# A fused two-block transformer kernel: convolution operands on SyncE's queue, forgetting bias through memory

## The reference, cut to what matters

```
# band attention of block one, 12 heads, two per pair
s = einsum(q, k) * scale + bias ; p = softmax(where(valid, s, -inf)) ; out = p @ v

# convolution module of the even mixer: 512 channels, 31 taps
a  = u * sigmoid(gate)
y  = conv_general_dilated(a, w, padding=[(CONV_K - 1, 0)], feature_group_count=512) + b
yf = (y - mean(y)) * rsqrt(var(y) + EPS) * ln_g + ln_b ; out = silu(yf)

# forgetting attention of the odd mixer: 16 heads
c  = cumsum(log_sigmoid(zf + b_f))
sc = einsum(q, k) / sqrt(Dh) + c[t] - c[s]
p  = softmax(where(t >= s, sc, NEG)) ; out = p @ v
```

## Time and profile before

| what | before |
| --- | --- |
| median of 3 runs | 1598.29 us (1597.94 to 1598.76) |
| the profiled execution | 1599.74 us |
| its span, first to last instruction | 1598.0 us |
| TensorE busy | 1587.4 us, 99% |
| VectorE busy | 1092.2 us, 68% |
| ScalarE busy | 919.5 us, 58% |
| GpSimd busy | 56.2 us, 4% |
| DMA | 287.67 MB, mean 180 GB/s |

### The profile page before, as it was taken

One profiled execution on the slowest core, in us unless ns is written; L12 is line 12 of the kernel. 1 busy time (PEld: TensorE's weight loads), 2 busy tenths in 40 slices (PEclk: granted clock), 3 DMA queues, 4 the chain that ended last, 5 costly groups with the idle time before them and its releaser, 6 DMA issues.

```text
span 1598.0 us, 23594 instructions
## 1 busy us (share of the span) xinstructions
PE 1587.4 (99%) x9256; PEld 1354.9 (85%) x9256; DVE 1092.2 (68%) x1759; ACT 919.5 (58%) x1555; POOL 56.2 (4%) x96
## 2 busy tenths in 40 slices
PE   9999999999999999999999999999999999999998
PEld 7898888889788888888887788888888889888887
DVE  5986867778677768656677466567565667775665
ACT  6766645567655546545476664447444484664544
POOL 4000000000030000000002100000000000000000
PEclk9999999999999999999999999999999999999999
DMA  8545675554355565566655555655666564356662
GB/s 299 146 146 189 217 238 192 186 174 144 118 193 190 175 199 179 188 197 189 191 159 161 143 191 186 196 185 171 210 185 188 181 200 146 119 184 199 184 189 75
DMA packets 212401, 287.67 MB, mean 180 GB/s; under 512 B 11100, under 2 KB 180382, under 8 KB 212292
## 3 DMA queue, kind: packets, MB, share of 16 engines
q1 hardware_dynamic: 208676, 280.00, 55.3%
q0 software_dynamic: 3616, 6.17, 1.4%
HBM read 284.47 MB, written 3.87 MB: 180 GB/s over the span
## 4 chain that ended last, share of the span: by engine, by line
PE 97%; DMA 1%; ACT 1%; issue 0%; SPq 0%; DVE 0%; POOL 0%; DVEq 0%; ACTq 0%
PE two L2216 91%; PE two L2293 1%; PE two L2462 1%; PE two L2475 1%; PE two L2485 1%; PE two L2870 0%; DMA vals<-u_dram 0%; PE two L2279 0%; PE two L2488 0%; DMA raw<-in_mem_w_kv 0%; PE two L2626 0%; DMA raw<-in_ffn_w_up 0%; DMA u_dram<-aux 0%; PE two L2456 0%; PE two L2844 0%
## 5 line engine op out<-in xcount | busy, mean ns | idle before, releaser
L2216 PE MATMUL two<-act_parts,w_hi 128*128 128x512 f32 (+1 forms) x2784 | 801.7, 353 | 0.0
L1488 DVE TENSOR_TENSOR w_lo<-raw,w_hi 128x1024 fp32r<-128x1024 f32 (+1 forms) x520 | 613.1, 1221 | 105.8 <-ACT w_hi L870 105.6
L2216 PE MATMUL two<-act_parts,w_lo 128*128 128x256 f32 x2256 | 635.0, 281 | 0.0
L2216 PEld LDWEIGHTS two<-act_parts,w_hi 128*128 128x128 f32 x2784 | 487.0, 188 | 81.1 <-issue 5.3
L870 ACT CAST w_hi<-raw 128x1024 fp32r<-128x1024 f32 (+1 forms) x522 | 516.6, 1046 | 5.5 <-DMA raw<-in_ffn_w_up 5.0
L2216 PEld LDWEIGHTS two<-act_parts,w_lo 128*128 128x128 f32 x2256 | 425.5, 189 | 2.1
L2216 PE MATMUL two<-w_hi,act_parts 128*128 128x512 f32 (+2 forms) x832 | 248.6, 378 | 1.5 <-ACT w_hi L870 1.2
L999 ACT COPY p_sb<-two 128x512 f32<-128x512 f32 x108 | 62.4, 578 | 247.1 <-PE two L2216 247.1
L2216 PE MATMUL two<-w_hi,hid_even 128*128 128x512 f32 x576 | 187.8, 393 | 0.0
L2216 PEld LDWEIGHTS two<-w_hi,act_parts 128*128 128x128 f32 x832 | 150.2, 188 | 33.4 <-issue 3.6
L1616 DVE TENSOR_TENSOR pt_sb<-two,p_sb 128x512 f32<-128x512 f32 x54 | 37.3, 691 | 198.4 <-ACT p_sb L999 198.4
(11 more groups left out here) (318 smaller groups left out, 1198.8 us busy)
## 6 DMA issues: line engine op xcount, KB each, us to landing
raw<-in_ffn_w_up SPq DMA_DIRECT2D x160, 512.0 KB, 3.9
raw<-in_ffn_w_down SPq DMA_DIRECT2D x132, 512.0 KB, 3.5
raw<-in_ffn_w_gate SPq DMA_DIRECT2D x80, 512.0 KB, 3.7
raw<-in_a_w_in SPq DMA_DIRECT2D x24, 512.0 KB, 4.3
raw<-in_fox_w_in SPq DMA_DIRECT2D x20, 512.0 KB, 3.8
raw<-in_ffn_w_up SPq DMA_DIRECT2D x32, 256.0 KB, 3.5
raw<-in_w_kv SPq DMA_DIRECT2D x12, 512.0 KB, 3.8
raw<-in_a_w_out SPq DMA_DIRECT2D x8, 512.0 KB, 3.8
```

The costliest lines, as they stand in the source:

```text
L1488: nc.vector.tensor_tensor(w_lo[:, r, 0:n], raw[:, r, 0:n], w_hi[:, r, 0:n], ALU.subtract).then_inc(lo_done, 1)
L2216: return nc.tensor.matmul(dst, a, w, start=start, stop=stop, skip_group_check=True)
```

## The change

**Convolution.** `stack` and the tile `shift` are gone: all four chunks are turned (`turn_u(0)` to `turn_u(3)`), copied (VectorE takes 0 and 2, ScalarE 1 and 3), written to `u_dram` and read back. Writes and reads stand on SyncE's queue, chunks 0 and 1 ahead of the load of the seventh slot of the output weights, chunks 2 and 3 ahead of the third load of the next feed-forward part. `conv(2)` and `conv(3)` stand ahead of `swa_out(0)`, `conv(1)` is cut by `values("swa", 2)`, and the last pair's scores come after the projection.

**Forgetting attention.** For pairs 2 to 7 (`BY_ROWS = 2`) the product with `pick` is left out. GpSimd's `spread_gates` writes `rowc` to `c_dram`, loads each pair's rows spread over all partitions into one of four buffers, cuts the causal mask into it (two `affine_select` per pair) and signals `bias_ready`. VectorE's `scores` waits for that and adds this tile in place of the mask. The three engines' lists go by stages: values of pair n-2, turns of n-1, scores of n.

**Band attention.** Some calls change places: scores of pair 3 before values of pair 1, values of pairs 2 and 3 together, values of 6 and 7 together behind two more output chunks; ScalarE's and VectorE's lists follow. Some semaphores are merged, with counts to match.

```diff
# SyncE
+            def stack_two(c):
+                if c == 0:
+                    sp.wait_ge(pad_out, 16 * CCH)
+                for i in (c, c + 1):
+                    sp.wait_ge(u_taken[i], 1)
+                    sp.dma_start(u_dram[i * P:(i + 1) * P, UPAD:UPAD + SEQ], cv[:, i, :]).then_inc(u_out[i], 16)
+                for i in (c, c + 1):
+                    sp.wait_ge(u_out[i], 16)
+                    for g in range(4):
+                        sp.dma_start(stacked(i, g),
+                                     bass.AP(tensor=u_dram.tensor, offset=(i * P + g * GRP) * (UPAD + SEQ) + UPAD - CONV_K,
+                                             ap=[[1, 4], [UPAD + SEQ, GRP], [1, XW]])).then_inc(stacked_in[i], 16)
+
+            out_rows("swa", ab_w_out_2[0], {6: lambda: stack_two(0)})
+            ffn(3, ffn_w_gate_2[0, 1], 0, ffn_w_up_2[0, 1], 0, ffn_w_down_2[0, 1], early={2: lambda: stack_two(2)})
...
# GpSimd: write_u and read_stacked removed (the same transfers for chunks 1 to 3)
+            def spread_gates():
+                pool.wait_ge(gates_m, 2)
+                pool.dma_start(c_dram, rowc[0:FOX_H, :]).then_inc(bias_in[0], 16)
+                pool.wait_ge(bias_in[0], 16)
+
+                def load(i):
+                    if i >= 4:
+                        pool.wait_ge(h_max, PAIR0["fox"] + BY_ROWS + i - 3)
+                    wide = FOX_BIAS[i % 4].rearrange("p (h k) -> p h k", k=CAUSAL)
+                    for at, n_keys in ((0, P), (P, SEQ)):
+                        pool.dma_start(wide[:, :, at:at + n_keys],
+                                       bass.AP(tensor=c_dram.tensor, offset=2 * (BY_ROWS + i) * SEQ,
+                                               ap=[[0, P], [SEQ, 2], [1, n_keys]])).then_inc(bias_in[i % 2], 16)
+
+                load(0)
+                load(1)
+                for i in range(FOX_H // 2 - BY_ROWS):
+                    pool.wait_ge(bias_in[i % 2], (0 if i % 2 else 16) + 32 * (i // 2 + 1))
+                    for half in range(2):
+                        own = FOX_BIAS[i % 4][:, half * CAUSAL:(half + 1) * CAUSAL].rearrange("p (a k) -> p a k", a=3)[:, 0:3:2, :]
+                        ins = nc.gpsimd.affine_select(out=own, in_=own, compare_op=ALU.is_ge, fill=NEG, base=0,
+                                                      pattern=[[0, 2], [-1, P]], channel_multiplier=1)
+                    ins.then_inc(bias_ready, 1)
+                    if i + 2 < FOX_H // 2 - BY_ROWS:
+                        load(i + 2)
...
# VectorE, scores
+                    elif kind == "fox" and n >= BY_ROWS:
+                        dve.wait_ge(bias_ready, n - BY_ROWS + 1)
...
# TensorE, scores
-                    if kind == "fox":
+                    if kind == "fox" and n < BY_ROWS:
...
# TensorE, band attention
             scores("band", 2)
+            scores("band", 3)
             values("band", 1)
...
-            values("band", 6)
             turns("band", 7)
             band_out(3, 1)
             band_out(5, 0)
+            values("band", 6)
+            values("band", 7)
             band_out(4, 1)
-            values("band", 7)
+            band_out(5, 1)
...
# TensorE, convolution and sliding window
+            project("GU1", 0, {3: [lambda: turns("swa", 0)], 6: [lambda: turn_u(0), lambda: turn_u(1), lambda: turns("swa", 1), lambda: values("swa", 0)]})
-            stack(0)
             scores("swa", 2)
             values("swa", 1)
-            stack(1)
-            project("GU1", 1, {3: [lambda: scores("swa", 3)]})
+            project("GU1", 1)
+            scores("swa", 3)
             conv(0, 0, QUADS // 2)
             turns("swa", 2)
             turn_u(2)
             turn_u(3)
             conv(0, QUADS // 2)
-            conv(1)
+            conv(1, 0, QUADS // 2)
             values("swa", 2)
+            conv(1, QUADS // 2)
             turns("swa", 3)
             mean(0)
+            conv(2)
+            values("swa", 3)
             mean(1)
-            values("swa", 3)
+            conv(3)
+            mean(2)
             swa_out(0, 1, 0)
             swa_out(0, 0, 0)
-            conv(2)
-            conv(3)
-            mean(2)
             mean(3)
...
# TensorE, forgetting attention
+            def fox_stages(n):
+                if n >= 2:
+                    values("fox", n - 2)
+                if n >= 1:
+                    turns("fox", n - 1)
+                if n < 8:
+                    fox_scores(n)
```

More of the change, by code:

```diff
@@ L518, in build @@
         gates_em = sem("gates_em")
+        bias_in = [sem(f"bias_in{i}") for i in range(2)]
+        bias_ready = sem("bias_ready")
         ml_bc = sem("ml_bc")
@@ L543, in build @@
         u_full = sem("u_full")
[L544 to L549, removed]
+        u_taken = [sem(f"u_taken{c}") for c in range(CCH)]
+        u_out = [sem(f"u_out{c}") for c in range(CCH)]
+        stacked_in = [sem(f"stacked_in{c}") for c in range(CCH)]
         cv_mu = sem("cv_mu")
@@ L1325, in _ @@
             exps("band", 7)
-            splits(139)
-            o_hi("band", 6)
             pt_copy("band", 7)
             splits(140)
+            o_hi("band", 6)
             o_hi("band", 7)
@@ L2109, in _ @@
             take_u(1, 0)
-            copy_stacked(0, 1)
             splits(284)
-            scores("swa", 3)
             probs("swa", 2)
@@ L2789, in _ @@
             turns("band", 3)
+            project("VB", 0)
             values("band", 2)
-            project("VB", 0)
+            values("band", 3)
             turns("band", 4)
-            values("band", 3)
             pe.wait_ge(fp_taken, PI["K2"] + 1)
@@ L2912, in _ @@
             project("GU0", 1)
-            project("GU1", 0, {3: [lambda: turns("swa", 0)], 6: [lambda: turns("swa", 1), lambda: turn_u(1), lambda: values("swa", 0)]})
-            stack(0)
+            project("GU1", 0, {3: [lambda: turns("swa", 0)], 6: [lambda: turn_u(0), lambda: turn_u(1), lambda: turns("swa", 1), lambda: values("swa", 0)]})
             scores("swa", 2)
             values("swa", 1)
-            stack(1)
-            project("GU1", 1, {3: [lambda: scores("swa", 3)]})
+            project("GU1", 1)
+            scores("swa", 3)
             conv(0, 0, QUADS // 2)
@@ L2934, in _ @@
             swa_out(0, 0, 0)
-            conv(2)
-            conv(3)
-            mean(2)
             mean(3)
-            for b in range(NTB):
-                swa_out(1, b)
-            variance()
-            for i in range(2, 4):
-                for b in range(NTB):
-                    swa_out(i, b)
+            swa_out(1, 0)
+            swa_out(1, 1)
+            out_chunk("swa", swa_ready, 2, 0, (0,))
+            variance()
+            out_chunk("swa", swa_ready, 2, 0, (1,))
+            swa_out(2, 1)
+            for b in range(NTB):
+                swa_out(3, b)
             for b in range(NTB):
@@ L3012, in _ @@
             fox_out(1, 1)
-            fox_scores(7)
-            for b in range(NTB):
-                fox_out(2, b)
-            turns("fox", 6)
-            for b in range(NTB):
-                fox_out(3, b)
-            turns("fox", 7)
-            values("fox", 6)
+            fox_out(2, 0)
+            fox_stages(7)
+            fox_out(2, 1)
+            fox_out(3, 0)
+            fox_out(3, 1)
             fox_out(4, 0)
+            fox_stages(8)
+            fox_out(4, 1)
             values("fox", 7)
@@ L3024, in _ @@
             out_end("fox", pair_ready("fox", 0), 0)
-            for i in range(4, NCH - 2):
-                fox_out(i, 1)
+            fox_out(5, 1)
             out_end("fox", pair_ready("fox", 0), 1)
```

235 lines of the change are left out of this document (97 added, 138 removed).

## The result

| | before | after |
| --- | --- | --- |
| median of 4 runs | 1598.51 us (1597.94 to 1598.76) | 1618.55 us (1617.28 to 1620.03) |
| ratio to before | | 1.0125, 95% interval 1.011 to 1.0141 |
| profiled execution, span | 1599.74, 1598.0 us | 1619.36, 1617.6 us |

The change costs 20 us. The sign was forecast, the size was not: 1618.55 lies well above the range, which ended at 1608.

What follows compares the result with a forecast made beforehand. TensorE, busy 99% of the span, was taken to bound the kernel. +7.2 (convolution) - 1.2 (band) - 0.8 (forgetting) = +5.2 on 1599.74 gave 1604.9, by the median 1603.5 us; range 1592.5 to 1608.

Steps and rivals of the forecast that it cites:

- Part 4: Forgetting attention: six bias products gone (1.1 us less), regrouping about equal, a PSUM wait of 0.3; sum -0.8 us.
- rival 3: Forgetting attention: bias late for pair 2, every pair waits 1 to 3 us, some 10 us on top; chance 0.05.
- Part 2: Convolution's operands through memory on SyncE's queue: TensorE waits; stage 7.2 us longer (4 to 10), removal of `stack` included.
- The line: Convolution: all eight reads of a pair of chunks queue at the same four engines; net near +5 us, chance 0.48.
- the steps: Convolution's transfer timetable: eight reads of 1.6 us from 859.7 to 872.5, loads until 878.0, chunk 2 landed 887.1, chunk 3 893.5.
- the upper end: Convolution: 1.8 us per read, stage 10 us longer, whole +8; unpriced clock loss in an 8 us TensorE wait left here.
- +9.1: Chunk 0 to the gates' sums: us added by the new transfers, from the stage's 7.2 with -1.9 ahead of chunk 0.
- Part 1: TensorE's convolution work: `stack` and the 1.36 us wait go, a turn comes; 3.1 us shorter without any new wait.
- part 3: Band attention: both 0.2 us waits covered and fewer changes between kinds of products; -1.2 us, from -1.6 to 0.
- Rival 1: Convolution: reads run side by side on more engines, nothing waits, 5.1 us won, 1593.2 us; chance 0.29.

Runs made afterwards that it cites:

- the bias alone: Kernel before with only the bias of forgetting pairs 2 to 7 through memory, lists in old order, some semaphores merged: 1598.25 us (0.9995).
- band attention alone: Kernel before with only the reordering of band attention: 1596.72 us (0.9986).
- the bias by product: Changed kernel with the bias of all eight forgetting pairs by TensorE's product again, new order of the lists kept: 1619.17 us (1.0128).
- the version by rows: Changed kernel with the reads of the convolution's operands having 32 rows outermost, 24 reads in place of 16, same queue and places: 1603.68 us (1.0031).

## Why the prediction was wrong, step by step

**Part 4, forgetting attention: the failed step.** It says that the stages "regroup the rest at about equal cost" and looks for new waits only at a place in PSUM. I followed TensorE's list and the bias, but not the two lists behind it: nowhere did I write down, for one pair, what VectorE and ScalarE do between the scores and the turns. In the new lists VectorE's split t+8 stands ahead of the probabilities and ScalarE's rounding of that slot behind the exponentials, so each pair's chain is longer by 2.8 us. TensorE's work hides some 2.2 of it in the middle of the stage and less at its ends. 6.2 us of waits and, in this execution, some 3.3 of reduced clock (an estimate: one less the granted clock, times the busy time, over the windows from 1348 to 1352 and 1396 to 1400) make the 9.45 us that stand against a forecast of -0.8. This is 10.3 of the 14.4 us between the forecast of the profiled run and its time. What the prediction did count there held: the removal of six products is worth 0.8 us (the bias alone, by its trace) where I took 1.1, and the bias is not late (rival 3).

**Part 2, the transfers: right mechanism, undersized.** The line at four engines came as forecast: reads alone ran at 95 GB/s or 1.5 us a read (I took 1.6), and the second eight took 13.3 us for the 12.8 of the steps. The mis-sized term is the first eight reads: 16.8 us for the same 12.8 (859.7 to 872.5). The prediction gave every read one price and put the loads behind the line; the loads ran beside the last reads, whose packets took up to twice as long. So chunk 1, for which I let TensorE wait 1 us, was awaited for 4.9, although the turns and the reads, like TensorE, came some 2 us sooner than in the steps. Chunk 2 came at 889.1 (forecast 887.1). The sum of TensorE's waits was 12.0 us where the steps give some 10.6 (1, 8 and some 1.5 for chunk 3). The other term is the clock: the prediction named it and put it in the upper end at no price, but the slower products behind the two waits add some 4 us. The 1.4 us of waits and these 4 make up most of the 5.7 us between the +9.1 and the +14.8; even the upper end, 1.8 us for every read, would have given only 3.2 more than +9.1. Two of the small sums don't come out of the terms beside them: 855.5, 0.4 and 2.1 make 858.0, not 858.5, and 1.0 more makes 859.0, not 859.7, so that by these terms the line would start 0.7 us earlier.

**Part 1 and part 3.** `stack` and the wait of 1.36 us went. From band attention alone to the whole change, chunk 0 comes 1.8 us earlier (866.77 to 864.94), where part 1 has 1.9 ahead of it. Band attention won 2.2 to 2.4 us by ratio and median, with an interval of 0.8 to 3.7, where I took 1.2; if that gain was sized too small, the error lay on the other side.

**The rivals.** Rival 1 came true only with 32 rows outermost, and with one wait of 1.5 us left: the gates' sums are then done at 1318.50, 4.7 us ahead of before, where parts 1 and 3 together gave 4.3. Its argument that the 128 partitions of the other side might spread the reads fell. No rival had a chain of attention made longer by the order of two lists, and so the range had no term for it.

## What to carry to other kernels

When calls are regrouped, write the chain of one unit (here: scores, maxima, exponentials, probabilities, turns) through every engine's list in the new order, and mark each entry of another unit that comes to stand inside it; a weight split that waits on another engine's list is such an entry. For a transfer, look at the outermost dimension: here reads with 4 outermost got a share of 0.27 of the engines, reads of the same bytes with 32 outermost nine tenths, and the loads behind them on SyncE's queue landed after 5.0 us in place of 12.5. The second form was worth 14.9 us although it needs 24 transfers in place of 16. A wait of TensorE can cost more than its length: here, products at half the clock stood behind four of the eight waits.

## What the runs showed of the hardware that I had not expected

- SyncE's issues took longer with narrow reads under way: 4.67 us for four reads and 4.78 for two writes, against 2.09 and 0.82 in the version by rows, which moves the same bytes.
- Reads that hold four engines were slower while loads ran beside them: 51 ns for a packet of 1136 bytes without loads, 64 to 104 ns with them.
- TensorE's granted clock was 0.50 to 0.65 behind waits of 1.9, 2.1, 4.9 and 7.1 us, while the wait of 1.36 us of before left it at 1.00, and so did one of 2.09 us with the bias by product. After waits of about 2 us it was sometimes lower and sometimes not; what decides, these runs don't tell. Where it was low, work went on at it for some 3 to 6 us.
- Work that nobody needs kept the clock up: 1.00 in place of 0.50 in the second wait and behind it, and chunk 2 in 3.6 us in place of 6.3. Whether the whole gets shorter (1616.87 against 1618.55 us by median) these times alone don't settle, and fill that ends after the operands come makes it longer (1621.78).
